# Two attentions rewritten: heads in pairs, mask added outside TensorE, projection units between the heads, and layer ends reordered

## What is computed

```python
def fox_attention(h, w_in, b_f, w_out):          # 16 heads of 64
    log_f = jax.nn.log_sigmoid(f_logit)
    c = lax.cumsum(log_f, axis=1).transpose(0, 2, 1)
    ...
        s = jnp.einsum('bhqd,bhkd->bhqk', qb, k, preferred_element_type=jnp.float32)
        s = s + cb[..., :, None] - c[..., None, :]
        s = jnp.where(k_pos[None, :] <= q_pos[:, None], s, NEG_INF)
        pr = jax.nn.softmax(s, axis=-1)
        return jnp.einsum('bhqk,bhkd->bhqd', pr.astype(v.dtype), v)
    ...
    return o @ w_out

def diff_attention(...):                         # 8 pairs of heads of 64, values of 128
    ...
        s = jnp.where(allowed[None, None], s, -jnp.inf)
        p = jax.nn.softmax(s, axis=-1).reshape(B, H, 2, Q_BLOCK, S)
        p = p[:, :, 0] - lam * p[:, :, 1]
        return jnp.einsum('bhqk,bkhe->bqhe', p.astype(v.dtype), v)
    ...
    o = rms_norm(o, subln_g, eps=SUBLN_EPS) * (1.0 - lam_init)
    return o.reshape(B, S, D) @ w_o
```

## Time and profile before

| | |
|---|---|
| time, median of 3 runs | 1733.32 us (1727.0 to 1733.7) |
| profiled execution, its own time | 1727.46 us |
| its span | 1725.7 us |
| PE, PEld busy | 94%, 79% |
| DVE, ACT, POOL busy | 56%, 43%, 9% |
| mean granted TensorE clock | 0.946 |

### The profile page before, as it was taken

The page is one execution under the profiler, slowest core; times in us unless marked ns, Lnnn a source line. Parts: engine busy times, 40 slices in busy tenths (PEclk is TensorE's granted clock), DMA queues, the critical chain, the costliest instruction groups (busy, mean ns, idle before and its releaser), DMA issues.

```text
span 1725.7 us, 23594 instructions
## 1 busy us (share of the span) xinstructions
PE 1623.6 (94%) x9478; PEld 1367.8 (79%) x9478; DVE 964.2 (56%) x1245; ACT 742.8 (43%) x962; POOL 163.2 (9%) x123
## 2 busy tenths in 40 slices
PE   8899899998899999978898999999999999999998
PEld 7765699986786999856677888868999785778997
DVE  5443465555574655558867566645555484545554
ACT  5332354445654544454642222135444563444442
POOL 1000101111101001110122122010000120010000
PEclk9975999999999999999889999999999997799999
DMA  7510265554463556544441000025547361045553
GB/s 268 154 61 1 85 214 187 192 184 134 142 200 113 199 195 193 162 138 129 145 134 61 1 2 2 1 76 185 179 157 234 135 195 38 16 143 189 184 172 115
DMA packets 81821, 229.12 MB, mean 133 GB/s; under 512 B 11728, under 2 KB 17552, under 8 KB 81712
## 3 DMA queue, kind: packets, MB, share of 16 engines
q1 hardware_dynamic: 81584, 227.54, 40.8%
q0 software_dynamic: 128, 0.07, 0.0%
HBM read 226.46 MB, written 1.05 MB: 132 GB/s over the span
## 4 chain that ended last, share of the span: by engine, by line
PE 62%; DVE 7%; ACT 4%; issue 1%; DMA 1%; POOL 1%; DVEq 0%; ACTq 0%; POOLq 0%; SPq 0%
PE PS L409 34%; PE PS L412 24%; PE PS L424 3%; ACT SH L381 2%; ACT ST L378 1%; DMA ST<-in_ffn_w_gu 1%; DVE LG L1469 1%; ACT XH L538 1%; DVE SL L384 0%; DVE XI L1187 0%; DVE XT L1477 0%; DVE XT L1478 0%; DVE X L641 0%; DVE SL L387 0%; DMA ST<-in_rw_w_k 0%
## 5 line engine op out<-in xcount | busy, mean ns | idle before, releaser
L387 DVE SCALAR_TENSOR_TENSOR SL<-ST,SM,SH 128x1024 fp32r<-128x1024 f32 (+1 forms) x240 | 294.9, 1247 | 167.6 <-ACT SH L381 131.6
L409 PE MATMUL PS<-XH,SH 128*128 128x256 f32 x1256 | 356.0, 283 | 3.8 <-DVE XL L1192 2.7
L412 PE MATMUL PS<-XH,SL 128*128 128x256 f32 x1256 | 356.3, 284 | 0.0
L409 PE MATMUL PS<-XL,SH 128*128 128x256 f32 x1256 | 355.4, 283 | 0.0
L381 ACT ACTIVATE SH<-ST,SM 128x1024 fp32r<-128x1024 f32 (+1 forms) x240 | 263.8, 1120 | 204.2 <-PE PS L412 125.6
L384 DVE TENSOR_TENSOR SL<-ST,SH 128x1024 fp32r<-128x1024 f32 (+1 forms) x167 | 214.7, 1298 | 180.1 <-ACT SH L381 157.0
L381 ACT ACTIVATE SH<-ST 128x1024 fp32r<-128x1024 f32 (+3 forms) x183 | 189.5, 1049 | 207.6 <-PE PS L412 182.0
L409 PE MATMUL PS<-SH,XH 128*128 128x512 f32 x576 | 237.5, 412 | 37.4 <-ACT JK L654 11.1
L409 PEld LDWEIGHTS PS<-XH,SH 128*128 128x128 f32 x1256 | 240.2, 191 | 5.4 <-ACT SH L381 4.2
L409 PEld LDWEIGHTS PS<-XL,SH 128*128 128x128 f32 x1256 | 237.7, 189 | 1.0
L412 PEld LDWEIGHTS PS<-XH,SL 128*128 128x128 f32 x1256 | 238.1, 190 | 0.2
(11 more groups left out here) (317 smaller groups left out, 1896.2 us busy)
## 6 DMA issues: line engine op xcount, KB each, us to landing
ST<-in_ffn_w_gu SPq DMA_DIRECT2D x80, 512.0 KB, 4.8
ST<-in_w_mlp_up SPq DMA_DIRECT2D x64, 512.0 KB, 4.4
ST<-in_w_mlp_down SPq DMA_DIRECT2D x64, 512.0 KB, 4.3
ST<-in_ffn_w_down SPq DMA_DIRECT2D x44, 512.0 KB, 4.2
ST<-in_w_attn_in SPq DMA_DIRECT2D x24, 512.0 KB, 4.7
ST<-in_w_conv_in SPq DMA_DIRECT2D x24, 512.0 KB, 4.5
ST<-in_w_ple_gate SPq DMA_DIRECT2D x16, 512.0 KB, 3.6
ST<-in_kv_w SPq DMA_DIRECT2D x16, 512.0 KB, 3.9
```

The source lines that it names most:

```text
L387: b = lo.do(lambda e: e.scalar_tensor_tensor(l[p0:p1, 0:cols], t[p0:p1, 0:cols], sc, h[p0:p1, 0:cols].bitcast(F32), ALU.mult, ALU.subtract ...
L409: pe.go(lambda e: e.matmul(o, l, r, start=start, stop=stop, skip_group_check=skip))
L412: return pe.do(lambda e: e.matmul(o, l, r, start=start, stop=stop, skip_group_check=skip))
```

## The change

The attention function is new. Heads go in pairs: the score matmuls of two heads alternate between the upper and lower 64 rows of the array. Mask and decay are no longer matmuls: `top` is one DVE instruction of each block (tensor_tensor_reduce), which writes the masked negated scores from PSUM to SBUF and their extreme to `NM`. The exps read SBUF. The weights are scaled by POOL. The product with V leaves the result transposed, so that `XH` and `XL` are split from it directly, and a unit of the output projection stands in each of the steps 4 to 11; the last V units stand in the first steps. The mask of the first attention, `MC`, has 384 columns for each of 16 heads: `CF` is written to a scratch tensor in HBM, read back to all 128 partitions, and two POOL additions put the causal part in. `top(0)` waits for it. In the second attention the norm goes over partitions: `norm1` copies and squares, `norm2` sums with a matmul of ones, so that every partition holds each token's sum, and raises `RR` of 128x256 to -0.5 on POOL, `norm3` multiplies. K takes banks 0 to 3 and V 4 to 7; the forget gate comes later; the first `row_scale` stands behind six units, and the one of ffn behind three more. `enter` has its units ahead before the transposes, without POOL, L378 or fillers.

```diff
@@ -586,12 +585,11 @@
 
         r = [None, None]
         chain(0)
+        ahead(2)
+        keep_busy(fill, tb[0][0])
+        r[0] = raw_half(0, tb[0])
         if between is not None:
             between()
-        keep_busy(fill[0], tb[0][0])
-        r[0] = raw_half(0, tb[0])
-        keep_busy(fill[1], banks[0])
-        ahead(2, po)
         chain(1)
...
+        def scores(j):
+            wait_banks([0, 1])
+            pe.wait(ready)
+            for qb, (c0, c1) in enumerate(blk):
+                for hl in range(2):
+                    r = slice(64 * hl, 64 * hl + 64)
+                    st[j, hl] = mm_t(bank(hl, c0, c1), QT[r, j, qb * 128:qb * 128 + 128], KT[r, j, 0:c1 - c0], True, True)
...
+        def top(j):
+            for hl in range(2):
+                h = 2 * j + hl
+                e_ = E[h % 6]
+                for qb, (c0, c1) in enumerate(blk):
+                    mk = mask(h)[:, c0:c1]
+                    t = ve.do(lambda e, hl=hl, c0=c0, c1=c1, e_=e_, mk=mk, k=2 * h + qb: e.tensor_tensor_reduce(
+                        e_[:, c0:c1], bank(hl, c0, c1), mk, -1.0, 3.0e38, ALU.add, ALU.min, NM[:, k:k + 1]),
+                        st[j, hl], t_mask, efree.get(h % 6))
+                bfree[hl] = t
+                st[j, hl] = t
+
...
+                for hl in range(2):
+                    h = 2 * j + hl
+                    for qb, (c0, c1) in enumerate(blk):
+                        w = po.do(lambda e, c0=c0, c1=c1, e_=E[h % 6], k=2 * h + qb: e.tensor_scalar(
+                            e_[:, c0:c1], e_[:, c0:c1], RI[:, k:k + 1], None, ALU.mult), y)
+                    wt[h] = w
+                return
+            z = ve.do(lambda e: e.tensor_scalar(NL[:, 2 * j:2 * j + 2], RI[:, 4 * j + 2:4 * j + 4], NLAM, None, ALU.mult), y)
+            for qb, (c0, c1) in enumerate(blk):
+                w = po.do(lambda e, c0=c0, c1=c1, qb=qb: e.tensor_scalar(
+                    PC[j % 2][:, c0:c1], E[2 * j % 6][:, c0:c1], RI[:, 4 * j + qb:4 * j + qb + 1], None, ALU.mult), y, pcfree.get(j % 2))
```

The norm and the steps of the new function (a single function now serves both attentions):

```diff
+        def norm1(j):
+            a = ac.do(lambda e: e.activation(OS[j % 2][:, :], bank(3, 0, 256), ACT.Copy), pv_[j], osfree.get(j % 2))
+            b = ac.do(lambda e: e.activation(OQ[:, :], bank(3, 0, 256), ACT.Square), pv_[j], os_.get(j - 1))
+            bfree[3] = b
+            os_[j] = b
+
+        def norm2(j):
+            wait_banks([3])
+            pe.wait(os_[j])
+            k = mm_t(bank(3, 256, 512), CC[:, C_ONE:C_ONE + 128], OQ[:, :], True, True)
+            os_[j] = k
+            a = ve.do(lambda e: e.tensor_scalar(RR[:, :], bank(3, 256, 512), 1.0 / 128, 1e-5, ALU.mult, ALU.add), k, rn_.get(j - 1))
+            bfree[3] = a
+            rn_[j] = po.do(lambda e: e.tensor_tensor(RR[:, :], RR[:, :], MHB, ALU.pow), a)
+
+        def norm3(j):
+            a = ve.do(lambda e: e.tensor_tensor(ON[:, :], OS[j % 2][:, :], RR[:, :], ALU.mult), rn_[j], on.get(j - 1))
+            osfree[j % 2] = rn_[j] = a
+            split_on(j, ON[:, :], a)
+
+        ks = list(ks)
+        pend = []
...
+            if s < 8:
+                scores(s)
+            if 3 <= s < 11:
+                pv(s - 3)
+            if s < 8:
+                top(s)
+            if diff and 4 <= s:
+                norm3(s - 4)
+            if 3 <= s < 11:
+                if diff:
+                    norm1(s - 3)
+                else:
+                    bfree[3] = split_on(s - 3, bank(3, 0, 256), pv_[s - 3])
+            flips = [] if not 2 <= s < 10 else [s - 2] if diff else [2 * s - 4, 2 * s - 3]
+            if flips:
+                flip(flips[0], ac)
+            if s < 8:
+                exps(s)
+            if 1 <= s < 9:
+                weights(s - 1)
+            half = None
+            if ks:
+                k = ks.pop(0)
+                half = half_unit(XS[0], k, OB, False, k == 7)
+                t0 = half(0)
+            elif s >= 4:
+                pe.wait(on[s - 4])
+                half = half_unit(XS[0], s - 4, OB, s == 4, s == 11)
+                t0 = half(0)
+            if len(flips) > 1:
+                flip(flips[1], ve)
+            if diff and 3 <= s < 11:
+                norm2(s - 3)
+            if half is not None:
+                if s < 9:
+                    t1 = half(1)
+                    ahead(1)
+                else:
+                    pend.append(half)
+                if s < 4 and not ks:
+                    vtok += evac_v([t0, t1])
+                    free.append(t1)
+        for half in pend:
+            t1 = half(1)
+            ahead(1)
+        return [t0, t1]
```

The mask, and the calls:

```diff
+    CF = ar("CF", 12, [16, S], F32, 2048)
+    a = ve.do(lambda e: e.tensor_scalar(CF[:, :], bank(6, 0, 256, 0, 16), -1.0, None, ALU.mult), t)
+    bfree[6] = a
+    scr = nc.dram_tensor("scr", (16, S), F32).ap()
+    MC = ar("MC", 9, [128, NH, 384])
+    t_c = dma_once(scr, CF[:, :], a, eng=po)
+    t_c = dma_once(MC[:, :, 128:384], scr.partition_broadcast(128), t_c, eng=po)
+    cm = CC[:, C_CM:C_CM + 128].unsqueeze(1).to_broadcast([128, NH, 128])
+    po.do(lambda e: e.tensor_tensor(MC[:, :, 0:128], MC[:, :, 128:256], cm, ALU.add), t_c)
+    t_mc = po.do(lambda e: e.tensor_tensor(MC[:, :, 256:384], MC[:, :, 256:384], cm, ALU.add))
...
+    t = attention(QT, KT, V0, [tq, tk], 0, lambda h: MC[:, h], t_mc, range(5, 8),
+                  lambda t: evac_a(V0, (4, 5, 6, 7), t, rt, scaled=True), [])
     last_pe = (pe.sem, pe.n)
...
             if g == 0:
                 continue
             if g > 1:
                 wait_banks(grp)
-            t = kind_b(XS[0], range(3 if g == 1 else 0, 8), grp, nblk=2 * n // 128, first=g > 1)
+            t = kind_b(XS[0], range(6 if g == 1 else 0, 8), grp, nblk=2 * n // 128, first=g > 1)
             if g == len(FG) - 1:
```

More of the change, by code:

```diff
@@ L376, in unit_split @@
             g = None
-        if g is not None and lo is po:
-            ready = ac.do(lambda e, g=g: e.activation(t[p0:p1, 0:cols], t[p0:p1, 0:cols], ACT.Copy, scale=GT[:, g:g + 1]), ready, t_gt)
-            g = None
         sc = 1.0 if g is None else GT[:, g:g + 1]
@@ L443, in kind_a @@
                     if lead and j == 0:
-                        pe.wait(xt[m])
+                        pe.wait(xt[m][0:2])
+                    elif xt is not None and not lead:
+                        pe.wait(xt)
                     for n in range(2):
@@ L668, in emit, with half_unit, half, attention @@
     ctx["finals"] = finals
-    def attention(QT, KT, V, tq, tk, tv, diff, aug, ON, after=None):
-        E = [ar(f"E{diff}{i}", 6, [128, 384], F32, 1536 * i) for i in range(4)]
-        PT = [ar(f"PT{diff}{i}", 7, [128, 384], F32, 1536 * i) for i in range(3)]
-        PC = [ar(f"PC{diff}{i}", *((7, [128, 384], F32, 1536 * (3 + i)) if i < 2 else (6, [128, 384], F32, 6144))) for i in range(3)]
+    def half_unit(xs, k, banks, first, last):
+        i, h, l = take_group(1, 0)[0]
+        tok = [None, None]
+        def half(m):
+            pe.wait(split_tok[i])
+            for n in range(2):
+                if first:
+                    pe.wait(bfree[banks[2 * m + n]])
+                ls = [x[:, k, m * 128:(m + 1) * 128] for x in xs]
+                rs = [x[:, n * 512:(n + 1) * 512] for x in (h, l)]
+                tok[m] = mm3(bank(banks[2 * m + n]), ls, rs, first, last)
+            if m:
+                pe_done[i] = tok[1]
+            return tok[m]
+        return half
+    def attention(QT, KT, V, ready, diff, mask, t_mask, ks, evac_v, free):
+        OB = (4, 5, 6, 7)
+        bufs = [ar(f"AB{diff}{i}", (6, 7, 8)[i // 5], [128, 384], F32, 1536 * (i % 5)) for i in range(15)]
+        E, PT, PC = bufs[0:6], bufs[6:10], bufs[10:12]
+        if diff:
+            OS = [ar(f"OS{i}", 13, [128, S], F32, 1024 * i) for i in range(2)]
+            OQ, RR = ar("OQ", 13, [128, S], F32, 2048), ar("RR", 13, [128, S], F32, 3072)
+            ON = ar("ON", 13, [128, S], F32, 4096)
+            MHB = MHW[:, 0:1].to_broadcast([128, S])
         NM = small(0, 32)
@@ L774, in pv @@
-        def pv(j):
-            if not diff:
-                return pv_t(j)
-            g, n = j // 2, j % 2
-            b = 6 + g % 2
-            if n == 0:
-                wait_banks([b])
-            pe.wait(pt[j], tv[0])
-            for qb in range(2):
-                for kb in range(qb + 1):
-                    t = 0 if qb == 0 else 1 + kb
-                    c = qb * 256 + n * 128
-                    k = mm_t(bank(b, c, c + 128), PT[j % 3][:, 128 * t:128 * t + 128], V[:, kb, j * 128:(j + 1) * 128], kb == 0, kb == qb)
-            ptfree[j % 3] = k
-            if n:
-                o = ON[:, :, g * 256:g * 256 + 256]
-                bfree[b] = ac.do(lambda e: e.activation(o, bank(b).rearrange("p (q c) -> p q c", q=2), ACT.Copy), k)
-                more.append(after(g, bfree[b]))
@@ L793, in attention @@
-        more = []
-        nj = 8 if diff else 16
-        step = 2 if diff else 1
-        for j in range(nj + 4):
```

(32 more changed lines are left out.)

288 lines of the change are left out of this document (107 added, 181 removed).

## The result

The changed kernel takes 1944.43 us (median, 1940.82 to 1947.1) against 1732.11 us before: 1.123 times as long, 95% interval 1.1199 to 1.1261. That is 212 us more. The prediction was 2024, range 1930 to 2085, slower.

What follows compares the result with a forecast made beforehand. The prediction took the kernel as bound by PE, at half clock in the first attention. From 1727.5 it took 46 (first attention), 30 (layer ends) and 9 (ffn) and added 382 (second attention): 2024, range 1930 to 2085.

Steps and rivals of the forecast that it cites:

- The step on the second attention: Second attention: each step holds an in-order cycle through a POOL power that PE can't pass; +382 us, 470 against 88.
- With hand-offs 5.8: Second attention: everything in a cycle other than the power takes 5.5 us, with hand-offs 5.8; a cycle is 56.0.
- 1.638 + 248 x 0.196 = 50.2 us: Second attention: price of one 128x256 power on POOL, extended from the 8-column time by the slope above 8 columns.
- The two slopes: Power on POOL: 0.196 us a column above 8 columns, 0.156 below, from traced powers of 1, 8 and 32 columns.
- The first rival: Second attention: a power has no price per column, about 0.75 us at 256 columns; total 1620; chance 0.11.
- The small slope: Second attention: a power costs 40.3 us by the smaller slope, 79 less in all; total 1945; chance 0.06.
- The rival of the other side: Second attention: the power has no price per column, so the kernel gets faster, 1620; chance 0.11.
- POOL shuts DVE out: Second attention: DVE's operations with two SBUF inputs stand still while a power runs, 24 us more, 2048; chance 0.05.
- First attention: Start to end of first output projection: earlier V, shorter steps at full clock, a mask wait; -46 us, between -58 and -20.
- PE never waits and yet runs at half speed: First attention's heads: PE busy 71.00 of 71.00 us at clock 0.52, on matmuls of 64 rows or 4.
- Layer ends: Eight layer ends: waits from ACT's scalings and POOL's slow splits go, and fillers at five; -30 us, between -41 and -20.
- ffn: ffn: three units before row_scale cover waits of 4.2 and 4.1 us, and a piece at half clock; -9 us.

Runs made afterwards that it cites:

- the widths: The changed kernel with the second attention's eight powers on 1, 8, 16, 32, 64, 128, 192 and 256 of the 256 columns: 1728.41 us.
- the last but one run: Kernel with small power, mask in pieces and norm's tiles freed early, now without splits behind the three held-back halves: 1605.55 us, 0.9298 of the kernel before.

## Why the prediction was right, and where it was off

**What decided.** The time lies within the range, but near its low end, 80 us under the 2024 that was given 0.69. What was right is the way it went and its cause. The step on the second attention held: a power on POOL is paid by the column, it stands in an in-order cycle, and PE can't pass it. The runs without a power and with an addition in its place show it by 338.5 and 335.6 us. "With hand-offs 5.8" was met exactly, 47.92 - 42.11 = 5.81. The mis-sized term is "1.638 + 248 x 0.196 = 50.2 us": a power took 41.7 on average. Eight times 8.5 is 68, and the stretch was predicted at 382 and came out at 317; the first power started 20 us after the first scores and not 15, which took 5 back. The slope went through the row of 32 columns, and that row holds 0.9 us that are no price of a column: in the earlier trace rows too the power begins at 1391.89 beside an operation of DVE,

```profile
1391.72 1.22 DVE L1805 TENSOR_TENSOR QK<-QK,QG 128x1024 f32<-128x1024 f32 x1
```

with two inputs in SBUF, 0.17 us ahead of it. Stretched over 248 columns, 0.9/24 became 9 us a power. The two slopes, 0.156 and 0.196, were the sign, and the power of 1.53 us for one column at 778.58 could have told why. The first rival had it in words, "part of 6.3 could be a start of some other kind". The small slope, a rival at 1945 with 0.06, was the true price. That the time came out at 1944 is in part luck: the powers took 41.7 and not its 40.3, 11 us more in all, and the gains elsewhere were 16 larger than predicted.

**The rival of the other side** (no price per column) fell, by the widths. **POOL shuts DVE out** fell in the form that was priced: `top` and the splits ran beside the powers. What there is of it goes the other way round, as the last section tells.

**First attention**, -51.9 for -46. The broadcast landed in 13.7 us where 14 was chosen, and the wait was 10.88 for 9; that 14, the middle of bounds of 5.6 and 22.4, came so close is luck. The fit of the Trainium skill (DMA: Bandwidth & Descriptors) gives an estimated 6.8 us for this transfer; the trace disagrees, with 13.7. The steps were priced too dear: 5.26 us instead of 7.1, since scores took 0.86 (not 1.8), the product with V 0.80 (not 1.5) and six transposes 0.56 of PE's time (not 1.0). The prediction let two heads share the array in part for the scores and not at all for the product with V; but 0.80 for two heads is what a single head takes in the run without decay, 114.59 - 113.80 = 0.79. Against that stand two waits that the prediction didn't have: 3.30 us for V's copy at 107.70, and 4.45 at the layer end, which counts in the next paragraph.
"PE never waits and yet runs at half speed" was the right reading, and the clock came back. The run without the decay matmuls shows the size: 36 us from nothing but two matmuls fewer a head, whose own time at half clock was 15.

**Layer ends**, -34.2 by the rows and 28.7 by the run that puts them back, for -30. The mechanism held: no wait for POOL's low part is left among the waits. The first of the eight ends was no gain but a loss of 1.7 us, for the reason that the last but one run removed.

**ffn**, -14.6 for -9. The waits of 4.2 and 4.1 fell to 0.18 each. The remaining 6.6 us I put down to the clock, which no longer falls behind the waits, but no run took that apart.

**The sum** thus had its large term too large by 65 and the gains too small by 16, and both errors went the same way: 2024 for 1944.

## What to carry to other kernels

Before moving a function of POOL from a few columns to a whole row, multiply its measured time per column by the new width, and take the slope from rows that had no neighbour at their start; a change that saves 100 us elsewhere can lose 330 in one line. Where a sum over partitions leaves the same row on all of them, do the costly function on tokens laid over partitions, two columns here, and spread the result with PE. When an instruction is late, look at what stands ahead of it on its own engine before freeing its tiles: here splits for later units did the harm, and one deleted line was worth 10 us.
